# One decoder layer on one core: score and value products of the attention heads regrouped on TensorE

## What is computed

```python
h = rms_norm(x, norm_mix)
qa, ka, va, qb, fb, ib, gb, qc, kc, vc = split(h @ w_in)      # 1024 x 3840
ya = dilated_attention(qa, ka, va, bias_a)    # 6 heads of 64
yb = hgrn2(qb, fb, ib, gb, ...)               # gated linear recurrence
yc = moba_attention(qc, kc, vc, bias_c)       # 6 heads of 64
x = x + concat(ya, yb, yc) @ w_out
x = x + (silu(conv(up_gate)) * conv(up_value)) @ w_down
x = x + sigmoid(rms_norm(x) @ w_pg) * (p @ w_pe)
return rms_norm(x, norm_final)
```

## Time and profile before

| | before |
|---|---|
| median of 3 executions | 793.18 us (792.83 to 793.69) |
| the profiled execution | 792.15 us, span of its core 790.3 us |
| TensorE busy | 770.8 us, 98% |
| VectorE, ScalarE, GpSimd busy | 454.4, 315.2, 119.7 us |
| granted TensorE clock, mean | 0.993 |
| start up to the end of unit 1 (0.00 to 28.17) | 28.17 us |
| recurrence, units 9 to 18 (68.26 to 156.08) | 87.82 us |
| attention ticks (156.08 to 318.97) | 162.89 us |
| w_up (353.69 to 593.98) | 240.29 us |
| w_down (593.98 to 718.06) | 124.08 us |

### The profile page before, as it was taken

How to read it: one execution, slowest core, us unless ns; L and a number is a source line. 1 busy time by engine, 2 the same in 40 slices (tenths; PEclk the granted TensorE clock), 3 DMA queues, 4 the chain that set the end, 5 groups by cost and what they waited for, 6 DMA issues and landing times.

```text
span 790.3 us, 10528 instructions
## 1 busy us (share of the span) xinstructions
PE 770.8 (98%) x3935; PEld 609.0 (77%) x3935; DVE 454.4 (58%) x705; ACT 315.2 (40%) x545; POOL 119.7 (15%) x97
## 2 busy tenths in 40 slices
PE   5999999999999999999999999999999999999994
PEld 4788778867777677788888888888888888887883
DVE  4754788475545442557677676677674333333554
ACT  7652223164444443345434334334333222326344
POOL 0030000044534342121110111101110000100000
PEclk9999999999999999999999999999999999999998
DMA  8332221311211110233332333323324332334202
GB/s 248 112 105 80 59 77 54 107 53 55 80 57 51 60 47 28 66 104 99 105 106 81 106 95 91 106 86 100 106 73 127 93 92 83 98 100 134 80 1 107
DMA packets 121744, 69.43 MB, mean 88 GB/s; under 512 B 2658, under 2 KB 118450, under 8 KB 121706
## 3 DMA queue, kind: packets, MB, share of 16 engines
q1 hardware_dynamic: 119982, 65.72, 28.4%
q10 hardware_dynamic: 1724, 3.19, 1.2%
HBM read 66.77 MB, written 2.13 MB: 87 GB/s over the span
## 4 chain that ended last, share of the span: by engine, by line
PE 96%; DMA 1%; ACT 1%; DVE 1%; issue 0%; SPq 0%; ACTq 0%; DVEq 0%
PE bank L459 28%; PE bank L461 26%; PE bank L460 26%; PE bank L594 4%; PE bank L568 2%; PE bank L566 2%; PE bank L499 2%; PE bank L580 2%; DMA raw<-in_w_in 1%; PE bank L533 1%; PE bank L553 0%; PE bank L516 0%; PE bank L766 0%; ACT scratch L959 0%; PE bank L510 0%
## 5 line engine op out<-in xcount | busy, mean ns | idle before, releaser
L459 PE MATMUL bank<-h_hi,w_hi 128*128 128x512 f32 (+1 forms) x664 | 268.4, 404 | 2.7 <-DVE h_lo L1155 2.7
L461 PE MATMUL bank<-h_hi,w_lo 128*128 128x512 f32 (+1 forms) x664 | 258.2, 389 | 0.0
L460 PE MATMUL bank<-h_lo,w_hi 128*128 128x512 f32 (+1 forms) x664 | 257.6, 388 | 0.0
L822 ACT ACTIVATE w_hi<-raw 128x1024 fp32r<-128x1024 f32 (+1 forms) x116 | 120.9, 1043 | 291.1 <-PE bank L461 291.0
L1149 DVE TENSOR_TENSOR w_lo<-raw,w_hi 128x1024 fp32r<-128x1024 f32 (+1 forms) x116 | 144.6, 1247 | 115.4 <-ACT w_hi L822 115.3
L459 PEld LDWEIGHTS bank<-h_hi,w_hi 128*128 128x128 f32 x664 | 125.0, 188 | 35.0 <-issue 6.2
L461 PEld LDWEIGHTS bank<-h_hi,w_lo 128*128 128x128 f32 x664 | 125.0, 188 | 26.4
L460 PEld LDWEIGHTS bank<-h_lo,w_hi 128*128 128x128 f32 x664 | 125.3, 189 | 23.5 <-issue 1.0
L1629 POOL TENSOR_SCALAR probs<-probs,row_inv 128x512 f32<-128x512 f32 (+3 forms) x48 | 66.0, 1375 | 187.5 <-DVE row_inv L1420 187.5
L461 PE MATMUL bank<-act_hi,w_lo 128*128 128x512 f32 x176 | 70.2, 399 | 0.0
L460 PE MATMUL bank<-act_lo,w_hi 128*128 128x512 f32 x176 | 69.4, 394 | 0.0
(11 more groups left out here) (185 smaller groups left out, 812.4 us busy)
## 6 DMA issues: line engine op xcount, KB each, us to landing
raw<-in_w_up SPq DMA_DIRECT2D x44, 512.0 KB, 3.8
raw<-in_w_in SPq DMA_DIRECT2D x30, 512.0 KB, 3.9
raw<-in_w_down SPq DMA_DIRECT2D x16, 512.0 KB, 3.5
raw<-in_w_out SPq DMA_DIRECT2D x8, 512.0 KB, 3.5
raw<-in_w_pg SPq DMA_DIRECT2D x8, 512.0 KB, 3.5
bias<-bias_table ACTq DMA_DIRECT2D x6, 512.0 KB, 4.3
...
```

What stands on the lines that cost most here:

```text
L459: pe.matmul(bank, hi, x_hi, start=first, stop=False)
L460: pe.matmul(bank, hi, x_lo, start=False, stop=False)
L461: return pe.matmul(bank, lo, x_hi, start=False, stop=last)
L822: act.activation(w_hi[:, u % SPLIT, 0:nk * ncol], raw[:, u % RAW, 0:nk * ncol], ACT.Copy)\
```

## The change

The steps are renumbered: `head_of(n)` and `tile_of(n)` now make steps 2j and 2j+1 the two heads of a pair for the same query block, so eight steps of a pair go through blocks 3, 3, 2, 2, 1, 1, 0, 0. `values_of_four(n)` takes the place of `step_values`: once in four ticks it issues the value products of four steps (two query blocks, both heads), the heads alternating instruction pair by instruction pair, and increments `weighted` once. `k_lo` becomes twice as large, one plane for each head, of which the other head's 64 rows are set to zero by GpSimd once at the start; L568's product then takes all 128 rows. `probs_t` has five buffers. The waits on `weighted` are rescaled. Small buffers are moved behind `r_row`, with pads of 128 and 160 bytes, and `under_setup` grows with `k_lo`.

```diff
--- before.py
+++ after.py
@@ -121,6 +121,7 @@
 SPLIT = 3
 TURN_LAG, VALUE_LAG = 4, 5
 PROBS = 5
+TURNED = 5
 
 
 V_UNITS = [g[2] for g in GROUPS if g[0] == "v"]
@@ -178,9 +179,14 @@
     return TICK_SLOTS[0] < slot < PROJ - 1
 
 
+def head_of(n):
+
+    return 2 * (n // (2 * TT)) + n % 2
+
+
 def tile_of(n):
 
-    return TT - 1 - n % TT
+    return TT - 1 - n % (2 * TT) // 2
 
 
 def rel_bucket(d):
@@ -229,6 +235,7 @@
             return ctx.enter_context(nc.semaphore(name))
 
 
+        sb("before_x", [P, 32])
         x_t = sb("x_t", [P, KT, SEQ])
         h_hi = sb("h_hi", [P, KT, SEQ], F32R)
         h_lo = sb("h_lo", [P, KT, SEQ], F32R)
@@ -237,15 +244,16 @@
         w_lo = sb("w_lo", [P, SPLIT, 1024], F32R)
         square = sb("square", [P, 4 * P])
         ident, ones, half_ones, flip = (square[:, i * P:(i + 1) * P] for i in range(4))
+        sumsq = sb("sumsq", [P, SEQ])
+        scratch = sb("scratch", [P, 4, SEQ])
+        r_row = sb("r_row", [P, SEQ])
         vec_cols = sb("vec_cols", [P, 4 * KT + 1])
         conv_cols = sb("conv_cols", [P, 4, 2 * FT])
         eps_col = sb("eps_col", [P, 1])
-        sumsq = sb("sumsq", [P, SEQ])
-        scratch = sb("scratch", [P, 4, SEQ])
-        r_row = sb("r_row", [P, SEQ])
         stat = sb("stat", [P, 4, TT])
         stat_bits = sb("stat_bits", [P, 2, TT], I32)
         parts = sb("parts", [P, TT, KT])
+        sb("after_small", [P, 40])
 
 
         mixing = ExitStack()
@@ -254,7 +262,7 @@
 
         q_both = sb("q_both", [P, 3, 2, SEQ], F32R, mixing)
         k_both = sb("k_both", [P, 3, 2, SEQ], F32R, mixing)
-        k_lo = sb("k_lo", [P, 3, SEQ], F32R, mixing)
+        k_lo = sb("k_lo", [P, 3, 2, SEQ], F32R, mixing)
         v_tok = sb("v_tok", [P, 3, TT, P], F32, mixing)
         v_t = sumsq
 
@@ -274,8 +282,7 @@
         mix_a_lo = sb("mix_a_lo", [P, PAIRS, SEQ], F32R, mixing)
         bias = sb("bias", [P, 2, 2, SEQ], F32, mixing)
         probs = sb("probs", [P, PROBS, SEQ], F32, mixing)
-        probs_t = sb("probs_t", [P, 4, SEQ], F32, mixing)
-        sb("beside_probs", [P, SEQ], F32, mixing)
+        probs_t = sb("probs_t", [P, TURNED, SEQ], F32, mixing)
         mix_b_hi = sb("mix_b_hi", [P, 2, SEQ], F32R, mixing)
         mix_b_lo = sb("mix_b_lo", [P, 2, SEQ], F32R, mixing)
         sb("under_gate", [P, 2, SEQ], F32, mixing)
@@ -285,7 +292,7 @@
         mixing.close()
 
         setup = ExitStack()
-        sb("under_setup", [P, 68 * 1024 // 4], F32, setup)
+        sb("under_setup", [P, 74 * 1024 // 4], F32, setup)
         x_rows = sb("x_rows", [P, TT, D], F32, setup)
         vec_rows = sb("vec_rows", [4 * KT + 1, P], F32, setup)
         conv_rows = sb("conv_rows", [2 * FT, 4, P], F32, setup)
@@ -338,7 +345,7 @@
         v_turned, v_ready = sem("v_turned"), sem("v_ready")
 
         z_chain, kin_arg, log_f, g_ready, kin_ready = (sem(s) for s in ("z_chain", "kin_arg", "log_f", "g_ready", "kin_ready"))
-        f_ready, tot_ready, corner_zero = sem("f_ready"), sem("tot_ready"), sem("corner_zero")
+        f_ready, tot_ready, corner_zero, k_lo_blank = (sem(s) for s in ("f_ready", "tot_ready", "corner_zero", "k_lo_blank"))
         gate_ready, bq_ready = sem("gate_ready"), sem("bq_ready")
         qk_ready, b_spread = sem("qk_ready"), sem("b_spread")
         b_scored, b_kept, b_out, b_squared = (sem(s) for s in ("b_scored", "b_kept", "b_out", "b_squared"))
@@ -554,18 +561,19 @@
                 mm.then_inc(v_turned, 1)
 
             def step_score(n):
-                head, i = n // TT, tile_of(n)
+                head, i = head_of(n), tile_of(n)
                 pair = head // 2
                 if n % (2 * TT) == 0:
                     pe.wait_ge(q_ready, 2 * (pair + 1))
                     pe.wait_ge(k_ready, 4 * (pair + 1))
                 if n >= 2:
                     pe.wait_ge(logits, n - 1)
+                if n == 0:
+                    pe.wait_ge(k_lo_blank, 2)
                 keys, hh, queries = (i + 1) * P, head % 2, slice(i * P, (i + 1) * P)
-                rows = slice(hh * HEAD, (hh + 1) * HEAD)
                 pe.matmul(score[n % 2][:, 0:keys], q_both[:, pair % 3, hh, queries], k_both[:, pair % 3, hh, 0:keys],
                           start=True, stop=False)
-                pe.matmul(score[n % 2][:, 0:keys], q_both[rows, pair % 3, hh, queries], k_lo[rows, pair % 3, 0:keys],
+                pe.matmul(score[n % 2][:, 0:keys], q_both[:, pair % 3, hh, queries], k_lo[:, pair % 3, hh, 0:keys],
                           start=False, stop=True).then_inc(scored, 1)
 
             def step_turn(n):
@@ -580,26 +588,30 @@
                     mm = pe.transpose(turned[n % 2][:, b * P:(b + 1) * P], probs[:, n % PROBS, b * P:(b + 1) * P], flip)
                 mm.then_inc(probs_turned, 1)
 
-            def step_values(n):
-                head, i = n // TT, tile_of(n)
-                pair, rows = head // 2, slice((head % 2) * HEAD, (head % 2 + 1) * HEAD)
-                pe.wait_ge(probs_t_ready, n + 1)
+            def values_of_four(n):
+
+                pair = n // (2 * TT)
+                pe.wait_ge(probs_t_ready, n + 4)
                 if n % (2 * TT) == 0:
                     pe.wait_ge(v_ready, 2 + pair + 1)
                     if pair < 2:
                         pe.wait_ge(b_normed, pair + 1)
                     else:
                         pe.wait_ge(mix_ready, pair - 1)
-                for jb in range(i + 1):
-                    mm = pe.matmul(outs[pair % 2][rows, i * P:(i + 1) * P], v_tok[:, pair % 3, jb, rows],
-                                   probs_t[:, n % 4, jb * P:(jb + 1) * P], start=(jb == 0), stop=(jb == i))
+                for step in (n, n + 2):
+                    i = tile_of(step)
+                    for jb in range(i + 1):
+                        for hh in range(2):
+                            rows = slice(hh * HEAD, (hh + 1) * HEAD)
+                            mm = pe.matmul(outs[pair % 2][rows, i * P:(i + 1) * P], v_tok[:, pair % 3, jb, rows],
+                                           probs_t[:, (step + hh) % TURNED, jb * P:(jb + 1) * P], start=(jb == 0), stop=(jb == i))
                 mm.then_inc(weighted, 1)
 
             def tick(m):
                 if 0 <= m - TURN_LAG < STEPS:
                     step_turn(m - TURN_LAG)
-                if m >= VALUE_LAG:
-                    step_values(m - VALUE_LAG)
+                if m >= VALUE_LAG and (m - VALUE_LAG) % 4 == 3:
+                    values_of_four(m - VALUE_LAG - 3)
                 if m < STEPS:
                     step_score(m)
 
@@ -621,7 +633,7 @@
                     if k == at:
                         tick(m)
                 if slot == TICK_SLOTS[-1] and k == LAST_VALUES:
-                    step_values(STEPS - 1)
+                    values_of_four(STEPS - 4)
                 if slot - 1 in V_UNITS and k == values_place(slot):
                     turn_values(slot - 1)
 
@@ -976,9 +988,9 @@
             def step_keep(n):
                 keys = (tile_of(n) + 1) * P
                 act.wait_ge(probs_turned, n + 1)
-                if n >= 4:
-                    act.wait_ge(weighted, n - 3)
-                act.activation(probs_t[:, n % 4, 0:keys], turned[n % 2][:, 0:keys], ACT.Copy).then_inc(probs_t_ready, 1)
+                if n >= TURNED:
+                    act.wait_ge(weighted, (n - TURNED) // 4 + 1)
+                act.activation(probs_t[:, n % TURNED, 0:keys], turned[n % 2][:, 0:keys], ACT.Copy).then_inc(probs_t_ready, 1)
 
             def bias_of(pair):
 
@@ -1289,7 +1301,7 @@
                 elif kind == "k" and 0 <= hh < 2:
                     dve.wait_ge(k_hi_ready, 2 * i + hh + 1)
                     dve.tensor_copy(k_both[other, i % 3, hh, :], k_both[own, i % 3, hh, :].bitcast(F32)).then_inc(k_ready, 1)
-                    dve.tensor_tensor(k_lo[own, i % 3, :], scratch[own, 1, :], k_both[own, i % 3, hh, :].bitcast(F32),
+                    dve.tensor_tensor(k_lo[own, i % 3, hh, :], scratch[own, 1, :], k_both[own, i % 3, hh, :].bitcast(F32),
                                       ALU.subtract).then_inc(k_ready, 1)
 
             def add_gated(f):
@@ -1398,13 +1410,13 @@
                 g = V_UNITS.index(unit)
                 dve.wait_ge(v_turned, g + 1)
                 if g >= 5:
-                    dve.wait_ge(weighted, 2 * TT * (g - 4))
+                    dve.wait_ge(weighted, 2 * (g - 4))
                 to = b_v[:, g, :, :] if g < 2 else v_tok[:, (g - 2) % 3, :, :]
                 dve.tensor_copy(to, turned[0][:, :].rearrange("p (t c) -> p t c", t=TT)).then_inc(v_ready, 1)
 
             def step_logits(n):
 
-                head, i = n // TT, tile_of(n)
+                head, i = head_of(n), tile_of(n)
                 pair, keys = head // 2, (i + 1) * P
                 if n % (2 * TT) == 0:
                     dve.wait_ge(bias_in[pair % 2], 16 * (pair // 2 + 1))
@@ -1420,7 +1432,7 @@
```

(8 more changed lines are left out.)

## The result

The changed kernel takes 750.09 us (median of 5 executions, 747.16 to 750.94), the kernel before 793.37 us beside it (5, 792.83 to 793.69). The ratio is 0.9453, with an interval of 0.9442 to 0.9465. The forecast was 746, the range 720 to 759, so the sign and the size are right; the kernel is 4 us slower than forecast. The profiled execution took 747.16 us with a span of 745.4 us; the other four are 2.9 to 3.8 us longer, and part of what follows is why.

The account below looks back on a forecast made before the run. TensorE, busy 770.8 of 790.3 us, was taken as the bound. Savings of 8.6 + 21.3 + 13.1 + 5.1 = 48.1 us, less 1 us for new waits, gave 793.2 - 47 = 746 us; range 720 to 759.

Parts of the forecast that it names:

- (a): Attention ticks, fewer value groups: 12 instead of 48 steps enter and leave the half-width tile; 8.6 us saved.
- (c): Value products, both heads side by side: alternating output halves take 0.0545 us per instruction instead of 0.109; 13.1 us saved.
- (b): Score products, k_lo at full height: no change of tile shape left around the second score product; 21.3 us saved.
- (d): Buffer addresses: products on act, mix and p no longer 32 bytes off a multiple of 64; 5.1 us saved.
- R2: Products on h gain from the address too: 710 us, or 728 at half the effect; chance 0.16.
- (e): The rest: memsets at the start, order of heads and tiles, fifth turned buffer, group waits; expected to cost nothing.
- R3: Attention ticks: TensorE waits for GpSimd in every tick, making the kernel slower than before, 805 us; chance 0.01.
- R1: Attention ticks: softmax chain comes late, GpSimd and VectorE holding each other up; 4 to 12 us, 750 to 758; chance 0.15.
- R4: Addresses: no gain for products on act, 751 us, or harm to those on h, 764; chance 0.08.
- What comes next in line: Steady heavy attention step: 7.5 us from score to transpose, softmax chain about 5.5, so some 2 us spare.
- The allowance for waits: Attention ticks: 1 us given back for new waits, because the softmax chain's spare time is thin.

Follow-up runs that it names:

- e1_klo_full: The kernel before with only k_lo in two zero-padded planes and the second score product over 128 rows; 776.77 us, ratio 0.9794.
- e2_addresses: The kernel before with only small buffers moved and two pads, so h, weights, act, mix and p start at multiples of 256 bytes; 788.79 us, ratio 0.9944.
- e5_changed_again: The changed kernel as it is, measured a second time; 748.66 us, ratio 0.9434.
- e12_norm_early: The changed kernel with b_norm's operations spread: first pair behind ticks 3, 4 and 5, second behind 7 to 10; 745.75 us, ratio 0.9398.

## Why the prediction was right, and where it was off

**(a) to (c), the stream of the ticks.** They were 8.6 + 21.3 + 13.1 = 43.0 us. The ticks lost 40.6 us from unit 18's end to unit 30's; with the 2.3 us of new waits taken out, the stream itself lost 42.9 us. A steady pair of units (heavy and light) went from 25.9 to 18.65 us, 7.25 less, and (a) to (c) are 43.0 / 6 = 7.17. The numbers of the steps hold one by one. Added up by kind over the ticks, the value products and the distances into them save 21.6 us, where (a) and (c) have 21.7; the scores, the transposes ahead of them and the products behind them save 20.9, where (b) has 21.3. L576 reads 128 rows at the distance of its columns; the 128-column score is at 0.14 us, inside its bounds of 0.06 to 0.23 and 0.03 above the 0.109 taken; e1_klo_full has (b) alone at 16.5 us; of the other 4.8, 36 x 0.10 are weights that are left uncovered behind each single value step in its order, and behind 12 groups here, and 1.0 is its late unit 21. Groups take 1.68 and 0.80 us, where "about 1.8 and 0.9" was written. The stage itself was misread from the sum: 43 less is 119.9, not "about 119", and 122.1 was measured.

**(c)'s reason was too narrow.** "The halves alternate, as in b_values" gives the right 0.0547 us, but strict alternation is not what it takes: six or eight in a row of each half lose only a third of the gain of a heavy group (2.16 us against 1.68 and 3.14), and 14 in a row still save 0.3.

**(d) has the right size and the wrong cause.** 5.1 us were forecast; e2_addresses measured 4.46 between the medians, and its units give the full 0.16 us each, with 0.7 given back ahead of `w_up`. But "32 bytes off a multiple of 64" is not what costs: with the weights off the same h products become slower, and with everything off nothing does. It is the difference of the two. R2, a gain for h, fell: units on h are at 5.44 in the changed kernel, as in the earlier trace rows. The Trainium skill (TensorE: Matmul & The Clock Gate, "Back-to-back issue gap") has 216 ns for an isolated product of 512 columns and about 131 ns for a sustained stream. The trace agrees with neither: no residue tried here gave less than 0.2267 us.

**(e), nothing, held.** TensorE waits for no memset, and from the start to the end of unit 18 the two profiles differ by 0.4 us. R3 fell with R1's premise, and R4 by the 5.44 us of both kinds of unit.

**What comes next in line held for the steady steps.** The prediction had 7.5 us from a wide step's score to its transpose, about 5.5 for the chain, and some 2 to spare. The step scored at 196.89 above is scaled and turned so:

```profile
200.60 1.79 POOL L1647 TENSOR_SCALAR probs<-probs,row_inv 128x512 f32<-128x512 f32 x1 [0.48 <-DVE row_inv L1432]
...
204.57 0.60 PE L588 MATMUL bank<-square,probs 128*128 128x128 f32 x4
```

That is 7.7 us, 5.5 and 2.2.

**The allowance for waits is the term that was too small.** "I give back 1 us for new waits" stood on GpSimd's chain as the thin place; the new waits measured 3.2 us (2.0 + 0.3 + 0.7 + 0.23). GpSimd was not it: its busy time is the same 65.99 us in the denser ticks, and TensorE waits for it once in them, 0.3 us. Its rows shifted both ways: over the whole stage those of 128 keys average 0.95 us instead of 1.27 (the earlier trace rows had 1.41 in a part of it), those of 384 keys 1.69 instead of 1.42. R1's other half, a late softmax chain, did come true once, at the first group, but through VectorE's normalization and ScalarE's queue. I had looked at one steady heavy step and not at the first group, which is the only one that meets `b_norm`. Its price was 2.0 us, in some executions 1.6 more for the lower clock behind it. A second small wait went unseen: `w_out` ends earlier than the chain that makes h and its sum of squares, which gives back 0.7 us at unit 38. A third, 0.23 us in unit 111, is in the changed kernel and all kernels made from it, not in e1_klo_full or e2_addresses. In the trace the transposes of the row before (L778) wait there for VectorE's sum (L1314), and that chain begins with a weight rounding on ScalarE (L834) that starts 0.79 us behind the end of the unit before instead of 0.49. Why it starts 0.3 us later stays open.

**The sum closes.** 792.15 - 48.1 + 2.0 + 0.3 + 0.7 + 0.23 = 747.3 us, and the profiled execution took 747.16. The median is 2.9 us higher, since most executions of the changed kernel have a lower mean clock than the profiled one (0.988 to 0.990 against 0.993). A stretch of 3.4 us at half clock lowers the mean over 745 us by 0.0023, so 0.988 is, as an estimate, two such stretches more than in the profiled execution. e5_changed_again's profile, at 0.988, has just these: one behind the pause, 1.6 us, and one more at the start, where the end of unit 0 varies by some 2 us. How much of the median is which is open, because a profile exists of one execution each. Without the wait, 793.2 - 48.1 + 0.9 = 746.0 us, and e12_norm_early measured 745.75. That the closing is within 0.3 us is in part luck, since the same kernel's medians lie 1.4 us apart in two measurements.
